# A 4-layer decoder step on one core: the residual given turned and loaded in eight pieces, and GLA's sample states as moving operand

## The chip, the cores and the metric

The kernel runs on one core of a Trainium2 chip. Its time is device microseconds (us) of one launch; the median of three runs is given. The engines are TensorE (PE; its weight loads are PEld), VectorE (DVE), ScalarE (ACT), GpSimd (POOL) and SyncE (SP), which issues most of the DMAs.

## What is computed

One inference step of a hybrid decoder for a prompt of 1024 tokens and a sample group of 8 sequences with 8 new tokens each, 1088 tokens in all, of width 1024. Layer 0 runs HGRN2 and latent attention beside each other, layer 1 gated linear attention (GLA); an MLP follows each. Everything is float32. The two places that the change touches are the input of the first projection and the GLA scan:

```python
hp = rmsnorm(xp, norm_mix[layer]); hs = rmsnorm(xs, norm_mix[layer])
hq, hf, hi, hg, cq, ckv, kr = _split(h @ w_in, EVEN_SPLIT)        # layer 0

def step(S, inp):                                                 # GLA, layer 1
    qb, kb, vb, gb = inp
    b = jnp.cumsum(gb, axis=2)
    o_inter = jnp.einsum('bhtk,bhkv->bhtv', qb * jnp.exp(b), S)
    ...
    o = o_inter + jnp.einsum('bhts,bhsv->bhtv', scores, vb)
    S_new = jnp.exp(b_last)[..., None] * S + jnp.einsum('bhsk,bhsv->bhkv', k_dec, vb)
```

For the sample group `S` comes in as `state_gla`: for each of 8 sequences and 4 heads a state of 128 keys by 256 values, met by the 8 queries of that sequence.

## The kernel before

The program is a row of stages, each with its own buffers and semaphores and a barrier of all engines at its end: load, even (the first projection), latent, attention, mix (HGRN2 and the sample attention), output projection, MLP, odd (the second projection), gla, output projection, MLP, store. Within a stage each engine has its own list of instructions, written out by hand, and waits on semaphores.

**The residual** lives on chip as `K.xT`, turned: 128 partitions by 8 pieces k by 1088 tokens. `load_stage` fetches the tokens row by row in nine tiles, on SP and ScalarE in turn, turns each in eight 128x128 pieces on TensorE, and ScalarE and VectorE copy them out. At the start of the even stage SP stores `K.xT` to DRAM as `K.x_save`, because the stage reuses its room for the latents; the output projection fetches it back.

**The first projection** multiplies in three parts: weights and x are split into a rounded high part and a low rest. ScalarE makes `x_hi` piece by piece (`high(act, k)`), VectorE `x_lo`. The first weight tile is in `K.first`, fetched during the load stage by `load_following`; the second, `raw[1]` (even_raw in the trace), is issued by SP as the first thing of the even stage. ScalarE splits it between `high` of k = 2 and k = 3. `first_two_groups` runs the first two groups of 128 outputs side by side, the second three pieces behind the first, and puts the sums of squares for the norm (`norm.pe`) in between. They need all seven additions on VectorE (`own.add`).

**GLA** runs four heads. In pass p (0 to 4) TensorE does the eight levels of head p, one a slot, each eight products of 128x128 (`level`, bank HB), and in the same slots the outputs of head p - 1: the values in slots 0 to 3, the sample values in slot 4, keys and state updates of the samples in slot 5, values turned and means in slot 6. In pass 4 there are no levels, and the sample values stand in slot 0. Small results share a ring of five PSUM banks, in the order of `banks_in_order`. The sample values of a head are, for each half of the 256 values, one product for the new tokens and eight with the states:

```python
for bi in range(NB):
    t = slice(bi * TS, (bi + 1) * TS)
    end = pe.matmul(out[:, t], s0[:, h % 2, bi, of], q_dec[:, SEQ + bi * TS:SEQ + (bi + 1) * TS],
                    start=False, stop=(bi == NB - 1))
```

Here the state is the stationary operand, 128x128, and 8 queries are the moving columns.

Of the kernel before, what the change touches and what calls it, by code (L numbers as in the profile page):

```python
# [20 lines left out]
ACT = mybir.ActivationFunctionType  # L21
# [3 lines left out]
P = 128  # L25
D = 1024
KD = D // P
# [105 lines left out]
def load_stage(nc, K, following):  # L133


    TILES = 9

    def rows(tile):
        return P if tile < 8 else NS

    with Stage(nc, "load") as s:
        xin = s.sb("xin", [P, TILES, D])
        tp = [s.ps(f"tp{i}", [P, 4, P]) for i in range(4)]
        const_in, ident_in, xin_in = s.sem("const_in"), s.sem("ident_in"), [s.sem(f"xin_in{i}") for i in range(TILES)]
        turned, following_in = s.sem("turned"), s.sem("following_in")
        copied_lo, copied_hi = s.sem("copied_lo"), s.sem("copied_hi")
        block = s.block()
        xp, xs = K.x_prompt, K.x_sample

        def fetch(eng, tile):  # L150
            src = xp[tile * P:(tile + 1) * P, :] if tile < 8 else xs
            eng.dma_start(xin[0:rows(tile), tile, :], src).then_inc(xin_in[tile], 16)

        @block.sync
        def _(sp):
            fetch(sp, 0)
            for tile in range(2, TILES, 2):
                fetch(sp, tile)
            load_following(sp, K, following, following_in)
            sp.wait_ge(following_in, 16)  # L160

        @block.gpsimd
        def _(pool):
            pool.memset(K.ones[:], 1.0)
            pool.memset(K.eps[:], EPS)
            with nc.allow_non_contiguous_dma(reason="a column of each norm weight, once"):
                for n, w in enumerate([K.norm_mix[0], K.norm_mlp[0], K.norm_mix[1], K.norm_mlp[1]]):
                    pool.dma_start(K.norms[:, n, :], w.rearrange("(k p) -> p k", p=P)).then_inc(const_in, 16)
            pool.wait_ge(const_in, 4 * 16)

        @block.tensor
        def _(pe):
            pe.wait_ge(ident_in, 16)
            for tile in range(TILES):
                n, i = rows(tile), tile % 2
                pe.wait_ge(xin_in[tile], 16)
                for half in range(2):
                    if tile >= 2:
                        pe.wait_ge(copied_lo if half == 0 else copied_hi, tile - 1)
                    for k in range(4):  # L180
                        c = (4 * half + k) * P
                        last = pe.transpose(tp[2 * i + half][:, k, 0:n], xin[0:n, tile, c:c + P], K.ident[0:n, 0:n])
                    last.then_inc(turned, 1)
            pe.wait_ge(copied_hi, 8)
            keep_running(pe, K, tp[3][:, 0, :], 4)

        def copy_out(eng, copy, half, copied):
            for tile in range(TILES):
                n = rows(tile)
                eng.wait_ge(turned, 2 * tile + half + 1)  # L190
                copy(K.xT[:, 4 * half:4 * half + 4, tile * P:tile * P + n], tp[2 * (tile % 2) + half][:, :, 0:n]
                     ).then_inc(copied, 1)

        @block.scalar
        def _(act):
            act.dma_start(K.ident[:], K.c_ident).then_inc(ident_in, 16)
            for tile in range(1, TILES, 2):
                fetch(act, tile)
            copy_out(act, lambda o, x: act.activation(o, x, ACT.Copy), 0, copied_lo)
# [4014 lines left out]
```

## Time and profile before

| | |
|---|---|
| median of three runs | 3082.57 us (3078.41 to 3083.43) |
| profiled execution | 3076.06 us, span 3074.3 us |
| mean TensorE clock | 0.989 of full speed |
| TensorE busy | 2978.1 us, 97% of the span |
| VectorE, ScalarE, GpSimd busy | 53%, 41%, 53% |
| moved by DMA | 451.91 MB, mean 147 GB/s |
| load stage | up to about 22 us |
| GLA stage | about 2076 to 2245 us |

The profile is of one execution. Times in it are from the start of the span; the time of the execution is the span and 1.8 us around it. A float32 matmul shows as two passes of TensorE, so counts of matmuls in the trace are twice those in the order of instructions, except for the turns against the identity. A clock of 1.00 is 2.4 GHz and 0.50 is 1.2 GHz.

### The profile page before, as it was taken

Reading aid. Unit: us, or ns where it says so; the run is one execution under the profiler, and the core shown is the slowest. Engines: PE = TensorE matmul, PEld = TensorE weight load, DVE = VectorE, ACT = ScalarE, POOL = GpSimd, SP = SyncE. Lnnn points to the kernel's source line nnn. Section 1 sums busy time; section 2 is a strip of 40 time slices with the busy share of each in tenths; the row PEclk is TensorE's granted clock in tenths of the full one; section 3 lists DMA queues with packets and bytes.
Section 4 is the critical chain, followed back from the end, with each engine's and each line's share of the span. In section 5 each row is a group of like instructions: output and inputs, shape, how many; then the busy total and the mean of one; then the engine's idle time right before and its main releaser. Section 6 shows DMA issues by size and latency. Waiting matters only on the chain. (4 is left out here: it accounts for less than half of the span.)

```text
span 3074.3 us, 55978 instructions
## 1 busy us (share of the span) xinstructions
PE 2978.1 (97%) x22805; PEld 2769.3 (90%) x22805; DVE 1631.1 (53%) x2254; ACT 1263.9 (41%) x2187; POOL 1639.1 (53%) x1375
## 2 busy tenths in 40 slices
PE   8999999999999999998999999999999999989998
PEld 7999667777777999998999989998899999989998
DVE  4122465566554374547666626734445644576665
ACT  4111435656654344344444452312444334344443
POOL 1122103455441167878999715731111687789995
PEclk9999999999999999999999999999999999999999
DMA  6222204667663134446344134657541444454442
GB/s 225 56 81 75 65 28 161 213 231 243 220 251 108 49 112 153 143 133 218 136 152 146 43 127 149 227 205 281 200 123 45 142 145 133 152 200 141 144 144 80
DMA packets 298127, 451.91 MB, mean 147 GB/s; under 512 B 18545, under 2 KB 195633, under 8 KB 297617
## 3 DMA queue, kind: packets, MB, share of 16 engines
q1 hardware_dynamic: 277152, 357.54, 34.6%
q0 software_dynamic: 20000, 88.64, 8.3%
q8 instruction: 182, 2.98, 0.4%
q10 hardware_dynamic: 720, 2.16, 0.2%
q14 instruction: 73, 0.59, 0.1%
HBM read 318.47 MB, written 129.81 MB: 146 GB/s over the span
## 5 line engine op out<-in xcount | busy, mean ns | idle before, releaser
L112 PE MATMUL mlp_X<-mlp_f_hi,mlp_w_hi 128*128 128x272 f32 x1968 | 568.7, 289 | 15.8 <-DVE xT L965 14.0
L113 PE MATMUL mlp_X<-mlp_f_lo,mlp_w_hi 128*128 128x272 f32 x1968 | 568.9, 289 | 0.0
L114 PE MATMUL mlp_X<-mlp_f_hi,mlp_w_lo 128*128 128x272 f32 x1968 | 568.1, 289 | 0.0
L809 POOL TENSOR_TENSOR mlp_w_lo<-mlp_raw,mlp_w_hi 128x256 fp32r<-128x256 f32 (+1 forms) x348 | 344.2, 996 | 162.2 <-ACT mlp_w_hi L693 120.8
L112 PEld LDWEIGHTS mlp_X<-mlp_f_hi,mlp_w_hi 128*128 128x128 f32 x1968 | 371.6, 189 | 18.4 <-DVE xT L965 16.3
L113 PEld LDWEIGHTS mlp_X<-mlp_f_lo,mlp_w_hi 128*128 128x128 f32 x1968 | 372.0, 189 | 0.0
L114 PEld LDWEIGHTS mlp_X<-mlp_f_hi,mlp_w_lo 128*128 128x128 f32 x1968 | 371.7, 189 | 0.0
L809 POOL TENSOR_TENSOR mlp_w_lo<-mlp_sums,mlp_w_hi 128x256 fp32r<-128x256 f32 (+1 forms) x276 | 299.7, 1086 | 14.5 <-ACT mlp_w_hi L693 11.1
L112 PE MATMUL mlp_Z<-mlp_f_hi,mlp_w_hi 128*128 128x272 f32 x976 | 281.3, 288 | 3.8 <-ACT mlp_ev L732 2.2
L113 PE MATMUL mlp_Z<-mlp_f_lo,mlp_w_hi 128*128 128x272 f32 x976 | 281.5, 288 | 0.0
L114 PE MATMUL mlp_Z<-mlp_f_hi,mlp_w_lo 128*128 128x272 f32 x976 | 281.0, 288 | 0.0
L965 DVE TENSOR_TENSOR xT<-xT,mlp_X 128x544 f32<-128x544 f32 x256 | 184.1, 719 | 141.6 <-PE mlp_X L114 140.2
L693 ACT ACTIVATE mlp_w_hi<-mlp_raw 128x256 fp32r<-128x256 f32 (+1 forms) x340 | 158.7, 469 | 207.9 <-PE mlp_X L114 125.0
L693 ACT ACTIVATE mlp_w_hi<-mlp_sums 128x256 fp32r<-128x256 f32 (+1 forms) x276 | 130.4, 480 | 228.9 <-POOL mlp_sums L809 128.5
L112 PEld LDWEIGHTS mlp_Z<-mlp_f_hi,mlp_w_hi 128*128 128x128 f32 x976 | 183.5, 188 | 5.0 <-ACT mlp_ev L732 2.6
L112 PE MATMUL odd_bank<-odd_x_hi,odd_w_hi 128*128 128x352 f32 (+1 forms) x552 | 181.5, 329 | 5.4 <-POOL odd_w_lo L3025 5.4
L113 PEld LDWEIGHTS mlp_Z<-mlp_f_lo,mlp_w_hi 128*128 128x128 f32 x976 | 183.8, 188 | 0.0
L114 PEld LDWEIGHTS mlp_Z<-mlp_f_hi,mlp_w_lo 128*128 128x128 f32 x976 | 183.6, 188 | 0.0
L114 PE MATMUL odd_bank<-odd_x_hi,odd_w_lo 128*128 128x352 f32 (+1 forms) x552 | 180.8, 327 | 0.0
L113 PE MATMUL odd_bank<-odd_x_lo,odd_w_hi 128*128 128x352 f32 (+1 forms) x552 | 180.6, 327 | 0.0
L112 PE MATMUL even_bank<-even_x_hi,even_w_hi 128*128 128x352 f32 (+1 forms) x504 | 166.3, 330 | 0.4 <-DVE even_w_lo L1312 0.4
L114 PE MATMUL even_bank<-even_x_hi,even_w_lo 128*128 128x352 f32 (+1 forms) x504 | 165.0, 327 | 0.0
(577 smaller groups left out, 7598.2 us busy)
## 6 DMA issues: line engine op xcount, KB each, us to landing
hidden<-mlp_ev SPq DMA_DIRECT2D x224, 272.0 KB, 2.2
mlp_f_lo_plain<-hidden SPq DMA_DIRECT2D x112, 544.0 KB, 5.5
mlp_raw<-in_w_down SPq DMA_DIRECT2D x64, 512.0 KB, 3.5
mlp_raw<-in_w_up SPq DMA_DIRECT2D x48, 512.0 KB, 5.6
projections<-odd_zout SPq DMA_DIRECT2D x24, 544.0 KB, 4.2
forms<-gla_f SPq DMA_DIRECT2D x20, 544.0 KB, 2.7
residual<-xT SPq DMA_DIRECT2D x2, 4352.0 KB, 15.1
projections<-even_zout SPq DMA_DIRECT2D x16, 544.0 KB, 3.2
```

What stands on the lines that cost most here:

```text
L112: pe.matmul(out, w_hi, x_hi, start=first, stop=False, skip_group_check=onto)
L113: pe.matmul(out, w_hi, x_lo, start=False, stop=False, skip_group_check=onto)
L114: return pe.matmul(out, w_lo, x_hi, start=False, stop=last, skip_group_check=onto)
L693: act.activation(slot(i)[0], src, ACT.Copy).then_inc(whi_done, 1)
L809: pool.tensor_tensor(to, x, y, op).then_inc(done_by, 1)
L965: dve.tensor_tensor(dst, dst, read_x(bank), ALU.add).then_inc(added, 1)
```

## The change

1. `kernel()` gives two more inputs: `x_turned`, the tokens laid out as `K.xT` is, and `c_norms`, the norm weights as columns. The load stage no longer turns anything. SP and ScalarE issue the eight pieces of 544 KB straight into `K.xT`, each with a semaphore of its own (`K.x_in[k]`) that the even stage takes over and waits for before `high(act, k)`. The first weights are issued first on SP and waited for in the even stage.
2. `K.x_save` is not written for the first layer; the output projection fetches from `x_turned` instead.
3. In GLA the operands of the sample states change places. `sample_queries` takes 32 columns of queries as stationary operand (8 of the sequence, 24 that follow and are not used) and the state's 256 values as moving ones. Four sequences go into the four quarters of a bank's partitions, eight matmuls in all. ScalarE copies the bank to `o_turned`, and `sample_values` turns and adds it with four matmuls against rows of the identity.

```diff
 def load_stage(nc, K, following):
     with Stage(nc, "load") as s:
...
+        const_in, filled = s.sem("const_in"), s.sem("filled")
+        K.first_in, K.x_in = s.carried("first_in"), [s.carried(f"x_in{k}") for k in range(KD)]
         block = s.block()
+        def fetch(eng, k):
+            eng.dma_start(K.xT[:, k, :], K.x_turned[:, k, :]).then_inc(K.x_in[k], 16)
 
         @block.sync
         def _(sp):
-            fetch(sp, 0)
-            for tile in range(2, TILES, 2):
-                fetch(sp, tile)
-            load_following(sp, K, following, following_in)
-            sp.wait_ge(following_in, 16)
+            load_following(sp, K, following, K.first_in)
+            for k in range(1, KD, 2):
+                fetch(sp, k)
+
+        @block.scalar
+        def _(act):
+            act.dma_start(K.norms[:], K.c_norms).then_inc(const_in, 16)
+            fetch(act, 0)
+            act.dma_start(K.ident[:], K.c_ident).then_inc(const_in, 16)
+            for k in range(2, KD, 2):
+                fetch(act, k)
+            act.wait_ge(const_in, 32)
...
-        @block.tensor
-        def _(pe):
-            pe.wait_ge(ident_in, 16)
-            for tile in range(TILES):
-                n, i = rows(tile), tile % 2
-                pe.wait_ge(xin_in[tile], 16)
...
@@ even_stage
             load(1)
-            sp.dma_start(K.x_save, K.xT[:]).then_inc(saved, 16)
...
+            act.wait_ge(K.first_in, 16)
             first.high(act, 0)
             for k in range(KD):
                 if k == 2:
                     first.high(act, 1)
                 if k == 3:
                     act.wait_ge(raw_in[1], 16)
                     split(1)
+                act.wait_ge(K.x_in[k], 16)
                 high(act, k, xhi_done)
...
@@ gla_stage
+                if p and i == sample_slot(p):
+                    uses.append((("oq", p - 1, 0), "A"))
                 if p and 0 <= i - value_slot(p, 0) < 4:
                     uses.append((("o", p - 1, i - value_slot(p, 0)), "A"))
...
+            def sample_queries(h):
+
+                b = bank(("oq", h, 0))
+                pe.wait_ge(cleared, 3)
+                pe.wait_ge(q_in, 16 * h + 16)
+                pe.wait_ge(s0_in, 16 * h + 16)
+                for m in range(2):
+                    for j in range(4):
+                        t0 = SEQ + (4 * m + j) * TS
+                        end = pe.matmul(b[QW * j:QW * (j + 1), m * V:(m + 1) * V], q_dec[:, t0:t0 + QW], s0[:, h % 2, 4 * m + j, :],
+                                        start=True, stop=True)
+                end.then_inc(filled, 1)
+
             def sample_values(h):
                 b = bank(("os", h, 0))
                 pe.wait_ge(a_out, L * h + L)
-                pe.wait_ge(q_in, 16 * h + 16)
-                pe.wait_ge(s0_in, 16 * h + 16)
+                wait_read(pe, ("oq", h, 0))
+                own_rows = K.ident[:].rearrange("p (j n) -> p j n", n=QW)[:, :, 0:TS]
                 for vc in range(VC):
                     out, of = b[:, vc * NS:(vc + 1) * NS], slice(vc * P, (vc + 1) * P)
                     pe.matmul(out, v_tok[0:NS, C, of], a[0:NS, h % 2, C, 0:NS], start=True, stop=False)
-                    for bi in range(NB):
-                        t = slice(bi * TS, (bi + 1) * TS)
-                        end = pe.matmul(out[:, t], s0[:, h % 2, bi, of], q_dec[:, SEQ + bi * TS:SEQ + (bi + 1) * TS],
-                                        start=False, stop=(bi == NB - 1))
+                    for m in range(2):
+                        end = pe.matmul(out[:, m * 4 * TS:(m + 1) * 4 * TS].rearrange("p (j n) -> p j n", n=TS), o_turned[:, m, of],
+                                        own_rows, start=False, stop=(m == 1))
                 end.then_inc(filled, 1)
...
+            def queries_out(h):
+                wait_filled(act, ("oq", h, 0))
+                if h:
+                    wait_filled(act, ("os", h - 1, 0))
+                act.activation(o_turned[:].rearrange("p m v -> p (m v)"), bank_of(("oq", h, 0))[:], ACT.Copy).then_inc(read_act, 1)
...
-                sp.dma_start(K.xT[:, SLOT[k], :], K.x_save[:, SLOT[k], :]).then_inc(x_back, 16)
+                sp.dma_start(K.xT[:, SLOT[k], :], K.x_turned[:, SLOT[k], :]).then_inc(x_back, 16)
```

The order of instructions on SP at the start of the program, before (xin are the token tiles, first the first weight tile):

```order
L152 DMA load_xin<-in_x_prompt 128x1024 x4
L152 DMA load_xin<-in_x_sample 64x1024
L371 DMA first<-in_w_in_even 128x8x128
L74 UNCONDITIONAL_BRANCH [waits load_following_in]
L1206 UNCONDITIONAL_BRANCH [waits barrier_Pool_Activation_PE_DVE_SP_release]
L1214 DMA even_raw<-in_w_in_even 128x8x128
L1224 DMA residual<-xT 128x8704
```

and of the change:

```order
L330 DMA first<-in_w_in_even 128x8x128
L141 DMA xT<-in_x_turned 128x1088 x4
L74 UNCONDITIONAL_BRANCH
L1166 UNCONDITIONAL_BRANCH [waits barrier_Pool_Activation_PE_DVE_SP_release]
L1174 DMA even_raw<-in_w_in_even 128x8x128
L1174 DMA first<-in_w_in_even 128x8x128 [waits even_lo_done]
```

The weights moved ahead of the tokens, even_raw follows four pieces of x in one queue, and the store of the residual is gone. ScalarE in the same place, of the change (w_hi is the high part of a weight tile):

```order
L319 ACTIVATE even_w_hi<-first 128x512 [waits load_first_in]
L297 ACTIVATE even_x_hi<-xT,norms 128x1088 [waits load_x_in0]
L297 ACTIVATE even_x_hi<-xT,norms 128x1088 [waits load_x_in1]
L319 ACTIVATE even_w_hi<-first 128x512
L297 ACTIVATE even_x_hi<-xT,norms 128x1088 [waits load_x_in2]
L1207 ACTIVATE even_w_hi<-even_raw 128x1024 [waits even_raw_in1]
L297 ACTIVATE even_x_hi<-xT,norms 128x1088 [waits load_x_in3]
```

The order is as it was; each piece now has a wait of its own. TensorE in GLA, around the last head's sample values, before (k_tok and v_own make the state updates):

```order
L3357 MATMUL gla_HB<-gla_f 128x128 x8
L3390 MATMUL gla_R<-gla_v_tok,gla_k_tok 128x256 x8
L3414 MATMUL gla_R<-gla_a,gla_v_tok 128x64
L3417 MATMUL gla_R<-gla_q_dec,gla_s 128x8 x8
L3414 MATMUL gla_R<-gla_a,gla_v_tok 128x64
L3417 MATMUL gla_R<-gla_q_dec,gla_s 128x8 x8
L3425 MATMUL gla_R<-gla_v_own,gla_k_tok 128x512 x4
```

and of the change, first around an inner head's, then around the last one's:

```order
L3380 MATMUL gla_R<-gla_s,gla_q_dec 32x256 x8
L3321 MATMUL gla_HB<-gla_f 128x128 x8
L3391 MATMUL gla_R<-gla_a,gla_v_tok 128x64
L3393 MATMUL gla_R<-ident,gla_o_turned 128x32 x2
```

```order
L3354 MATMUL gla_R<-gla_v_tok,gla_k_tok 128x256 x8
L3380 MATMUL gla_R<-gla_s,gla_q_dec 32x256 x8
L3391 MATMUL gla_R<-gla_a,gla_v_tok 128x64
L3393 MATMUL gla_R<-ident,gla_o_turned 128x32 x2
L3391 MATMUL gla_R<-gla_a,gla_v_tok 128x64
L3393 MATMUL gla_R<-ident,gla_o_turned 128x32 x2
L3401 MATMUL gla_R<-gla_v_own,gla_k_tok 128x512 x4
```

A level product (HB) stands between queries and values in the inner heads, and nothing in the last.

## Rows read from the trace of the kernel before

**Rows 1.** The page: span and busy time.

```profile
span 3074.3 us, 55978 instructions
PE 2978.1 (97%) x22805; PEld 2769.3 (90%) x22805; DVE 1631.1 (53%) x2254; ACT 1263.9 (41%) x2187; POOL 1639.1 (53%) x1375
```

**Rows 2.** Stretches: length, busy by engine PE to POOL, clock, DMA share, GB/s.

```profile
2.00:20.00 18.00, 10.61 (x65) 9.55 (x66) 4.84 (x7) 5.87 (x9) 3.02 (x4) 1.00 0.94 278
46.43:51.46 5.03, 5.03 (x15) 3.80 (x16) 0.00 (x0) 1.92 (x3) 2.15 (x1) 0.66 0.01 3
```

**Rows 3.** Timeline of SP's queue (start us, us, engine, line): first weights.

```profile
3.52 0.61 SPq L371 DMA_DIRECT2D first<-in_w_in_even  x1
```

**Rows 4.** DMA issues of the first 24 us: KB, us to landing.

```profile
first<-in_w_in_even SPq DMA_DIRECT2D x1, 512.0 KB, 16.8
...
even_raw<-in_w_in_even SPq DMA_DIRECT2D x1, 512.0 KB, 4.3
```

**Rows 5.** Timeline of ScalarE, 22 to 56 us; in brackets idle before.

```profile
22.73 0.63 ACT L360 ACTIVATE even_w_hi<-first 128x512 fp32r<-128x512 f32 x1 [1.93 <-PEq L76]
...
27.08 1.04 ACT L1249 ACTIVATE even_w_hi<-even_raw 128x1024 fp32r<-128x1024 f32 x1
28.02 5.57 ACT L338 ACTIVATE even_x_hi<-xT,norms 128x1088 fp32r<-128x1088 f32 x5
...
51.69 0.31 ACT L309 ACTIVATE even_rstd<-even_sum,eps 128x64 f32<-128x64 f32 x1 [2.13 <-PE even_sum L301]
```

**Rows 6.** Timeline of VectorE, 22 to 56 us.

```profile
30.51 1.22 DVE L1312 TENSOR_TENSOR even_w_lo<-even_raw,even_w_hi 128x1024 fp32r<-128x1024 f32 x1
...
36.70 9.68 DVE L332 TENSOR_TENSOR acc<-acc,even_sq 128x1088 f32<-128x1088 f32 x7
54.47 1.88 DVE L1329 TENSOR_TENSOR even_zout<-even_bank,even_rstd 128x384 f32<-128x384 f32 x4 [8.10 <-ACT even_rstd L312]
```

**Rows 7.** Timeline of TensorE, 42 to 64 us: the first sums.

```profile
46.43 2.41 PE L301 MATMUL even_sum<-acc,ones 128*128 128x512 f32 x4 [2.49 <-DVE acc L332]
```

**Rows 8.** Stretches of GLA from each head's sample values on, columns as before.

```profile
2120.89:2130.38 9.49, 9.49 (x54) 9.28 (x53) 0.70 (x1) 0.45 (x2) 2.44 (x1) 0.64 0.18 59
2163.09:2171.00 7.91, 7.91 (x53) 7.75 (x53) 0.70 (x1) 0.45 (x2) 2.48 (x1) 0.78 0.50 198
2203.72:2212.72 9.00, 9.00 (x63) 8.64 (x62) 1.41 (x2) 0.89 (x3) 2.48 (x1) 0.81 0.20 64
2226.75:2239.62 12.87, 12.87 (x74) 10.76 (x73) 9.80 (x15) 6.15 (x8) 1.46 (x2) 0.73 0.32 119
```

**Rows 9.** Timeline of TensorE in GLA, head 1's sample values and after.

```profile
2163.09 0.43 PE L3414 MATMUL gla_R<-gla_a,gla_v_tok 64*128 64x64 f32 x2
2163.46 1.95 PE L3417 MATMUL gla_R<-gla_q_dec,gla_s 128*128 128x8 f32 x16
2165.34 0.43 PE L3414 MATMUL gla_R<-gla_a,gla_v_tok 64*128 64x64 f32 x2
...
2167.51 3.66 PE L3357 MATMUL gla_HB<-gla_f 128*128 128x128 f32 x16
2171.00 1.15 PE L3369 MATMUL gla_R<-ident,gla_k_dec 128*128 128x128 f32 x9
```

**Rows 10.** Timeline of TensorE in GLA: another level product.

```profile
2139.05 1.95 PE L3357 MATMUL gla_HB<-gla_f 128*128 128x128 f32 x16
2140.84 1.46 PE L3390 MATMUL gla_R<-gla_v_tok,gla_k_tok 128*128 128x256 f32 x6
```

**Rows 11.** Timeline of TensorE in the first output projection.

```profile
956.63 0.64 PE L3840 MATMUL evenout_A<-mla_acc,evenout_sel 128*32 128x256 f32 x8
957.20 0.64 PE L3842 MATMUL evenout_A<-mla_rows_new,evenout_pnT 64*32 64x256 f32 x8
```

**Rows 12.** Lines L3840 and tile gla_R: ns of one, min/median/max.

```profile
L3840 PEld LDWEIGHTS evenout_A<-mla_acc,evenout_sel x8: 106/108/109, 956.6 to 956.7; 128*32 128x32 f32 x8
L3840 PE MATMUL evenout_A<-mla_acc,evenout_sel x8: 379/391/403, 956.6 to 956.9; 128*32 128x256 f32 x8
...
L3498 ACT ACTIVATE gla_v_tok<-gla_R x16: 591/602/617, 2087.1 to 2218.7; 128x512 f32<-128x512 f32 x16
```

More of the change, by code:

```diff
@@ L133, in load_stage @@
 def load_stage(nc, K, following):
-    TILES = 9
-    def rows(tile):
-        return P if tile < 8 else NS
     with Stage(nc, "load") as s:
[L142 to L146, printed above, removed]
+        const_in, filled = s.sem("const_in"), s.sem("filled")
@@ L162, in _ @@
+        @block.scalar
[6 more added lines that the diff above has]
+            act.wait_ge(const_in, 32)
         @block.gpsimd
         def _(pool):
[L164 to L168, printed above, removed]
@@ L169, in _ @@
-            pool.wait_ge(const_in, 4 * 16)
-        @block.tensor
-        def _(pe):
-            pe.wait_ge(ident_in, 16)
-            for tile in range(TILES):
-                n, i = rows(tile), tile % 2
-                pe.wait_ge(xin_in[tile], 16)
[L177 to L199, printed above, removed]
@@ L201, in _ @@
-        @block.vector
-        def _(dve):
-            copy_out(dve, lambda o, x: dve.tensor_copy(o, x), 1, copied_hi)
+            pool.memset(K.ones[:], 1.0).then_inc(filled, 1)
+            pool.memset(K.eps[:], EPS).then_inc(filled, 1)
+            pool.wait_ge(filled, 2)
 def store_stage(nc, K):
@@ L1194, in even_stage @@
         M.z_stored = [16 * len(STORED[i::2]) for i in range(2)]
-        saved, following_in, const_in, weight_in = (s.sem(n) for n in ("saved", "following_in", "const_in", "weight_in"))
+        following_in, const_in, weight_in = (s.sem(n) for n in ("following_in", "const_in", "weight_in"))
         lat_squared, lat_added, lat_mean, lat_logged, lat_rstd, lat_normed = (s.sem(n) for n in (
@@ L1240, in _ @@
                 store(g - 2)
-            sp.wait_ge(saved, 16)
             sp.wait_ge(const_in, 16 * 8)
@@ L1319, in evacuate @@
                 if g in LATENT:
-                    if c == 0 and g == LATENT[0]:
-                        dve.wait_ge(saved, 16)
                     dst = K.xT[:, g - LATENT[0], t0:t0 + tn]
@@ L3115, in gla_stage @@
     ITEMS, FB, RB = L + 1, G.FB, 5
+    QW = 32
     K_DEC, Q_DEC = len(LEVELS), len(LEVELS) + 1
@@ L3436, in _ @@
                 for i in range(SLOTS):
+                    if p and i == sample_slot(p):
+                        sample_queries(p - 1)
                     if p < HEADS:
@@ L3515, in roots @@
                 act.activation(rstd[:], rstd[:], ACT.Exp, scale=-0.5).then_inc(rstd_out, 1)
+            def queries_out(h):
[3 more added lines that the diff above has]
+                act.activation(o_turned[:].rearrange("p m v -> p (m v)"), bank_of(("oq", h, 0))[:], ACT.Copy).then_inc(read_act, 1)
             for p in range(HEADS + 1):
                 for i in range(SLOTS):
+                    if p and i == sample_slot(p):
+                        queries_out(p - 1)
                     if p and 0 <= i - value_slot(p, 0) < 4:
@@ L4166, in constants, with turned_tokens, norm_columns @@
                 c_unit=(i % 32).astype(f)[:, None])
+def turned_tokens(x_prompt, x_sample):
+    rows = np.concatenate([x_prompt[0], x_sample.reshape(NS, D)])
+    return rows.reshape(T, KD, P).transpose(2, 1, 0)
+def norm_columns(norm_mix, norm_mlp):
+    return np.stack([norm_mix[0], norm_mlp[0], norm_mix[1], norm_mlp[1]]).reshape(4, KD, P).transpose(2, 0, 1)
 OUTPUTS = dict(y_prompt=(1, SEQ, D), y_sample=(NB, TS, D), mla_rows_prompt=(1, 1, SEQ, LAT),
@@ L4206 @@
     nc = bacc.Bacc("TRN2", target_bir_lowering=False, num_devices=1)
-    arrays = {f"in_{n}": np.ascontiguousarray(x) for n, x in {**inputs, **constants()}.items()}
+    arrays = {f"in_{n}": np.ascontiguousarray(x) for n, x in {
+        **inputs, **constants(), "x_turned": turned_tokens(inputs["x_prompt"], inputs["x_sample"]),
+        "c_norms": norm_columns(inputs["norm_mix"], inputs["norm_mlp"])}.items()}
     a = {n[3:]: nc.dram_tensor(n, x.shape, mybir.dt.from_np(x.dtype), kind="ExternalInput").ap()
```

12 lines of the change are left out of this document (6 added, 6 removed).

## The prediction

> **What bounds the kernel now.** I read the page first: TensorE is busy for 2978 of 3074.3 us [rows 1]. So a change counts only where TensorE waits, runs at the lower clock, or has instructions removed. Then I read the timeline and the DMA queues of the first 56 us, and the GLA stage by timeline and by stretches: the two places that the diff touches.
>
> The profiled execution took 3076.06 us, 6.5 us under the median 3082.57 of the runs shown. I sum against it and take the difference off the median. A measurement of this kernel can tell about 0.2%, 6.2 us, from no change.
>
> The start is bound by transfers: from 2 to 20 us the DMA engines are 0.94 busy at 278 GB/s [rows 2], and the first weights, issued last, land at 3.52 + 16.8 = 20.3 us [rows 3, 4]. ScalarE begins the projection at 22.73 us, splits the second weight tile at 27.08 and from 28.02 us makes x_hi for k = 3 and on [rows 5]. From there VectorE has no gap: w_lo to 31.73, x_lo, then seven additions from 36.70 to 46.38 us [rows 6]. TensorE waits 2.49 us for the last of them, until 46.43 us [rows 7]. The five microseconds behind that wait have a mean clock of 0.66: 3.4 us of them at 1.2 instead of 2.4 GHz [rows 2]. The root follows the 64-column sum at their end (Ln at 51.69, VectorE again at 54.47) [rows 5, 6].
>
> In GLA nothing waits at the sample states. But the stretches that hold them, 9.49, 7.91, 9.00 and 12.87 us long and fully busy, have mean clocks of 0.64, 0.78, 0.81 and 0.73 [rows 8]. In head 1 the sample values take 2163.09 to 2167.51 = 4.42 us: twice two passes for the new tokens and 16 passes of 8 moving columns (a matmul in fp32 is two passes in the trace). The level product behind them, 16 passes, takes 3.49 us [rows 9] where it takes 1.79 elsewhere [rows 10]. TensorE is occupied there but streams few columns, and the lower clock follows.
>
> **Start, part by part.** Removed: 72 transposes and 18 copies. They lie under the transfers and are worth nothing in themselves. The 4352 KB store of the residual goes too; nothing on TensorE waited for it: 0.
> Moved: the eight pieces of the residual and the first weights are issued from the first microsecond, and the projection takes each as it lands. Two places of the order matter. On SP the second weight tile (even_raw) is issued behind the first weights and four pieces. On ScalarE the split of that tile stands ahead of x_hi for k = 3. So k = 0, 1 and 2 go early, and everything from k = 3 on waits for even_raw, the last tile of the whole load.
> When does it land? By 20.3 us 64 + 4352 + 512 KB were in. Now 528 KB more stand ahead of its end (the tile itself, and the norms in one piece): 540,672 B / 278 GB/s = 1.9 us, so 22.2 us. GpSimd's gather of the norms leaves the same engines; no row prices it alone, and I allow 0.3 us: 21.9. Bounds: 20.3 if the longer rows move that much faster, and 24.6 if the tile starts only when all else is in and then takes the 4.3 us that it takes now [rows 4].
> The split then starts at 22.0 instead of 27.08 us [rows 5]. The chain behind it, ScalarE's x_hi and VectorE's x_lo and additions, keeps its spacing: **5.1 us** (2.4 to 6.7 by the bounds).
> The new wait leaves TensorE idle from about 15 to 24 us; queued behind it are the rest of both groups and the sums. I expect it back at 1.2 GHz. Between 31.73 and 43.94 us (46.43 - 2.49) it has 12.2 us of work at full clock [rows 6, 7]. If it loses what it loses behind the present wait, half of 3.4 us, the 2.49 us wait for the additions covers that. Most of that wait is then gone, and I take the drop of the clock behind it as gone too: 5.03 x (1 - 0.66) = **1.7 us**. Its other end is 0.
>
> **GLA, part by part.** Out of each head go 32 passes of 8 columns. In come eight matmuls with 32 stationary and 256 moving columns, a copy on ScalarE, and four matmuls of 32 columns against the identity.
> The output projection has the same shape as the eight: 128*32 by 256 over the four quarters of the array's columns, eight passes, start to start 956.63 to 957.20 = 0.57 us [rows 11]. Eight matmuls are 16 passes: 1.14 us. The four narrow ones are eight passes with a full stationary tile; nearest are the 8-column ones, 16 in 1.88 us, 0.117 each: 0.94. The new tokens' stay at 4.42 - 2 x 1.88 = 0.66 [rows 9]. Sum 2.74 against 4.42: 1.7 us a head, **6.7 us**.
> The copy of 512 columns takes 0.60 us [rows 12]. For heads 0 to 2 a level product of 1.79 us stands between queries and values and hides it. The last head has none, as the order rows show: there the copy costs its 0.60 and two handovers, which I estimate at 0.2 each: **-1.0 us** (0.6 to 1.4). Behind the waiting TensorE stand the state updates and the last values; VectorE and ScalarE wait for those. The ring of five banks gets one more user a head; the banks behind it keep their predecessors: 0. The fill of 24 columns on GpSimd at the stage's start lies under the first loads: 0.
> Clock: lost time is length x (1 - clock): 3.4 + 1.7 + 1.7 + 3.5 = 10.3 us [rows 8]. The run of few columns shrinks from 4.42 to 1.60 us (0.94 + 0.66) with a level product on either side, so I take the losses of heads 0 to 2 as gone (6.8). In the last head a wait of 1.0 us, narrow matmuls and updates of 32 rows follow one another; there I take half, 1.7. Together **8.5 us**, bounds 0 and 10.3.
>
> One rule speaks against the eight matmuls. The Trainium skill (TensorE: Matmul & The Clock Gate, "The mechanism") says that a weight load overlaps matmuls in flight only where its row group differs, and these share one. The trace disagrees for this shape: eight passes with their loads took 0.57 us, and eight loads of 108 ns in a row would be 0.86 [rows 11, 12]. By the row the four heads save 6.7 us, by the rule nothing.
>
> **Sum.** 5.1 + 1.7 + 6.7 - 1.0 + 8.5 = 21.0 us. 3076.1 - 21.0 = 3055.1 for a profiled execution; 3082.6 - 21.0 = 3061.6, say **3062 us**, for the median.
>
> **Rivals.**
> 1. *The clock still falls behind the sample values.* For it: eight narrow passes remain, and in head 0 the clock was down for most of its 9.49 us [rows 8]. Against: the run is 2.8 times shorter. Gain 21.0 - 8.5 = 12.5: 3070 us. Chance 0.15.
> 2. *The start gives little.* The tile lands at 24.6 us and the cold restart outlasts its cover: 2.4 us and no clock back. Gain 2.4 + 14.2 = 16.6: 3066 us. For it: the tile is last in the longer of two queues. Chance 0.15.
> 3. *Loads not hidden in the narrow tiles*: 16 x 0.108 = 1.7 us a head [rows 12], which eats what is saved. Gain 21.0 - 6.9 = 14.1: 3068.5 us. Chance 0.04. This is the mechanism of the skill's rule named above.
> 4. *Slower.* The array empties between the column quarters, so each of the 16 passes costs its full 0.39 us [rows 12]: 6.3 instead of 1.14 us a head, -20.5 in all, and sparse streaming keeps the lower clock, -8.5. That gives -8.0: 3090.6 us. It decides from a pass of 0.26 us on, where 12.5 us are spent. The 0.57 us for eight stands against it. Chance 0.02.
> 5. *More*: the last head keeps 2.4 GHz too, and the tile lands at 20.3: 21.0 + 1.8 + 1.6 = 24.4: 3058 us. Chance 0.12.
> The forecast itself has 0.52.
>
> **How the numbers follow.** The time is the forecast's, 3062; its own range, with the spread of the runs (3078.4 to 3083.4), is 3058 to 3066. Eight in ten takes in rivals 2, 3 and 5 and about half of 1: 3055 to 3070. All cases but rival 4 gain over 6.2 us: faster 0.94 with something unseen allowed for, 0.04 within, 0.02 slower.
>
> **What would show it.** Right: the split of even_raw at about 22 us with a DMA as its releaser; TensorE's wait ahead of the first sum under 1.5 us and the clock at 1.00 behind it; 16 passes of 32 by 256 in about 1.1 us; a wait of about 1 us for the copy in the last head alone; the level product behind the sample values 1.8 us long in heads 0 to 2. Wrong: even_raw after 24 us; clocks under 0.9 behind the sample values; TensorE waiting elsewhere in GLA, since each head now needs its items, gate and queries some 3 us sooner.

## The result and the profile after

| | before | after |
|---|---|---|
| median of 5 runs | 3082.48 us (3078.41 to 3083.43) | 3065.70 us (3063.49 to 3069.54) |
| ratio, 95% interval | | 0.9946 (0.9934 to 0.9958) |
| profiled execution | 3076.06 us | 3069.54 us |

The change made the kernel 16.8 us faster; 21 were forecast. The profiled execution of after is the slowest of its five runs, so the two profiles lie only 6.5 us apart. The page of after:

```profile
span 3067.8 us, 55744 instructions
...
PE 2965.6 (97%) x22693; PEld 2749.4 (90%) x22693; DVE 1624.0 (53%) x2245; ACT 1264.4 (41%) x2182; POOL 1635.5 (53%) x1372
```

TensorE's busy time fell by 12.5 us [rows 1], its passes from 22,805 to 22,693: four heads lose 32 narrow ones and gain 16 and 8, 32 fewer in all, and most of the rest are the load's 72 turns.

The start, after. SP's queue:

```profile
0.75 0.44 SPq L330 DMA_DIRECT2D first<-in_w_in_even  x1
...
9.09 0.38 SPq L1174 DMA_DIRECT2D even_raw<-in_w_in_even  x1
```

Stretches, as in [rows 2]:

```profile
4.00:14.00 10.00, 4.71 (x20) 4.74 (x21) 2.54 (x3) 4.89 (x6) 2.42 (x3) 1.00 1.04 407
22.00:24.00 2.00, 2.00 (x8) 1.81 (x7) 2.00 (x3) 2.00 (x3) 0.00 (x0) 0.50 0.00 0
24.00:26.00 2.00, 2.00 (x12) 2.00 (x11) 2.00 (x3) 2.00 (x3) 0.00 (x0) 0.84 0.00 0
38.00:40.00 2.00, 2.00 (x3) 0.94 (x4) 0.00 (x0) 0.70 (x2) 2.00 (x1) 0.57 0.00 0
40.00:42.00 2.00, 2.00 (x5) 1.04 (x4) 0.00 (x0) 0.98 (x2) 0.12 (x1) 0.58 0.00 0
```

ScalarE, VectorE (additions, then the copying out of the even stage) and TensorE (the sums), in this order:

```profile
18.62 1.06 ACT L1207 ACTIVATE even_w_hi<-even_raw 128x1024 fp32r<-128x1024 f32 x1 [3.80 <-DMA even_raw<-in_w_in_even]
19.58 5.56 ACT L297 ACTIVATE even_x_hi<-xT,norms 128x1088 fp32r<-128x1088 f32 x5
```

```profile
28.25 9.67 DVE L291 TENSOR_TENSOR acc<-acc,even_sq 128x1088 f32<-128x1088 f32 x7
46.12 2.75 DVE L1287 TENSOR_TENSOR even_zout<-even_bank,even_rstd 128x384 f32<-128x384 f32 x6 [8.20 <-ACT even_rstd L271]
```

```profile
37.98 3.52 PE L260 MATMUL even_sum<-acc,ones 128*128 128x512 f32 x4 [1.92 <-DVE acc L291]
```

The same ten microseconds of the kernel before:

```profile
4.00:14.00 10.00, 6.11 (x29) 5.69 (x30) 1.81 (x3) 2.77 (x4) 1.02 (x2) 1.00 1.00 306
```

The transfers run at 407 GB/s where they ran at 306; from 2 to 20 us it is 339 against the 278 of [rows 2]. ScalarE takes even_raw at 18.62 us, a DMA its releaser; before it was 27.08 [rows 5]. The additions come 8.45 us earlier (28.25 for 36.70) and the copying out 8.35 us, 46.12 for 54.47 [rows 6]. TensorE still waits 1.92 us ahead of the sums, for 2.49 [rows 7]. It also comes back from its wait for the tile at the lower clock (0.50 from 22 to 24 us) and runs at it again from 38 to 42.

GLA, after: TensorE around the sample states of an inner head.

```profile
2123.02 1.07 PE L3380 MATMUL gla_R<-gla_s,gla_q_dec 128*32 128x256 f32 x16
2124.02 2.05 PE L3321 MATMUL gla_HB<-gla_f 128*128 128x128 f32 x16
2126.00 0.43 PE L3391 MATMUL gla_R<-gla_a,gla_v_tok 64*128 64x64 f32 x2
2126.36 0.63 PE L3393 MATMUL gla_R<-ident,gla_o_turned 128*128 128x32 f32 x4
...
2127.76 2.03 PE L3321 MATMUL gla_HB<-gla_f 128*128 128x128 f32 x16
2129.62 0.27 PE L3333 MATMUL gla_R<-ident,gla_k_dec 128*128 128x128 f32 x1
```

The 16 passes of queries take 2123.02 to 2124.02 = 1.00 us, own tokens and narrow passes 2126.00 to 2127.76 = 1.76. The level product behind them takes 1.86 us where it took 3.49 [rows 9]. The stretches of the inner heads from each one's queries on, and two of the last head's end:

```profile
2123.00:2133.00 10.00, 10.00 (x81) 7.82 (x81) 2.36 (x5) 3.34 (x8) 2.49 (x1) 1.00 0.49 163
2160.00:2170.00 10.00, 10.00 (x83) 7.87 (x81) 1.96 (x4) 3.16 (x7) 2.50 (x1) 1.00 0.81 296
2198.00:2208.00 10.00, 10.00 (x81) 7.76 (x80) 2.30 (x4) 3.28 (x8) 2.50 (x1) 1.00 0.19 57
2230.00:2235.00 5.00, 3.79 (x34) 3.60 (x33) 2.27 (x4) 2.40 (x5) 0.00 (x0) 1.00 0.61 210
2235.00:2240.00 5.00, 3.78 (x18) 3.81 (x19) 3.48 (x4) 3.80 (x5) 0.00 (x0) 0.66 0.38 110
```

The clock is whole in the heads where it fell to 0.64, 0.78 and 0.81 [rows 8], and falls once at the very end. The last head's copy, with ScalarE's row between TensorE's:

```profile
2219.79 1.07 PE L3380 MATMUL gla_R<-gla_s,gla_q_dec 128*32 128x256 f32 x16
...
2221.03 0.58 ACT L3499 ACTIVATE gla_o_turned<-gla_R 128x512 f32<-128x512 f32 x1
...
2221.75 0.40 PE L3391 MATMUL gla_R<-gla_a,gla_v_tok 64*128 64x64 f32 x2 [0.89 <-ACT gla_o_turned L3499]
```

TensorE waits 0.89 us for it.

To see where the rest went, I read the same anchors in every trace: the starts of the first and last matmul on a stage's tile. Lengths in us. "before" and "changed" are means of three profiles each, "later split" of three kernels with that edit (experiment 4):

| stretch | before | changed | later split |
|---|---|---|---|
| start to the query latents | 301.3 | 293.1 | 289.3 |
| to the first keys of the mix | 195.6 | 196.7 | 196.6 |
| mix | 440.6 (439.0 to 442.3) | 446.9 (445.7 to 448.1) | 441.9 (440.6 to 443.7) |
| to the even output | 7.4 | 7.1 | 7.1 |
| to the odd projection | 821.1 | 823.6 | 822.6 |
| to GLA | 310.3 | 310.7 | 310.1 |
| GLA, to the output's first matmul | 172.2 | 159.1 | 159.1 |
| to the last store's turns | 819.1 | 819.2 | 818.4 |

Two places gain, 8.2 and 13.1 us. The attention mix, whose code is the same, gives 6.3 us back, and the stretch to the odd projection 2.5. The mean spans of the profiled executions, 3076.2 and 3065.8 us, lie 10.4 us apart; the medians show 15 to 17.

### The profile page after: what moved, and what is told of

Its sections match the earlier page's. It is cut to its first block and busy times, and to the rows that moved or that the text cites. A ratio compares the mean times of both kernels' runs of the same rounds, so it can differ in the third digit from the quotient of the medians.

```text
span 3067.8 us, 55744 instructions
## 1 busy us (share of the span) xinstructions
PE 2965.6 (97%) x22693; PEld 2749.4 (90%) x22693; DVE 1624.0 (53%) x2245; ACT 1264.4 (41%) x2182; POOL 1635.5 (53%) x1372
## 5 line engine op out<-in xcount | busy, mean ns | idle before, releaser
L112 PE MATMUL mlp_X<-mlp_f_hi,mlp_w_hi 128*128 128x272 f32 x1968 | 569.1, 289 | 13.5 <-DVE xT L924 11.6
L112 PEld LDWEIGHTS mlp_X<-mlp_f_hi,mlp_w_hi 128*128 128x128 f32 x1968 | 371.8, 189 | 16.0 <-DVE xT L924 13.9
```

The lines of the kernel that those rows point to most:

```text
L112: pe.matmul(out, w_hi, x_hi, start=first, stop=False, skip_group_check=onto)
```

## The experiments

All times are medians. Each group was run on one chip beside the kernel before.

**1. The two halves of the change, each alone, and sample states split in two.** The kernel before took 3078.59 us here.

gla_only is the kernel before with the change's parts in `gla_stage` alone:

```diff
+    o_turned = s.sb("o_turned", [P, 2, V])
...
+                        sample_queries(p - 1)
...
+                        queries_out(p - 1)
```

> Only the GLA part of the change; load and projection as before. In the changed kernel's profile the GLA stage (first level product to the last) is 12 us shorter, 6 of it instructions and 6 to 8 clock. Theory A (the parts add up, and what is missing from the whole is a number of drops of the clock elsewhere that differs by execution, 1.7 us each): 12 us under before, 3070.5, with 0.00 to 3 drops in the mix stage. Theory B (the shift of the start causes the drops of the clock in mix): 12 us as well, but with mix at a clock of 1.00 as in the profile of before, since nothing ahead of GLA moved.

Measured: 3068.80 us, ratio 0.9969 (0.9957 to 0.9981), so -9.8 us (-13.2 to -5.8). GLA is 159.6 us long, 0.6 more than with the whole change. The mix is 442.2 us long and has two drops of the clock, at 589 and 811 us, although nothing ahead of GLA moved. That speaks against Theory B.

start_only is the rest: turned residual, pieces and waits, with GLA as before:

```diff
+            load_following(sp, K, following, K.first_in)
+            for k in range(1, KD, 2):
+                fetch(sp, k)
```

> Only the start of the change (turned residual in pieces, norms as columns); GLA as before. VectorE's first evacuation was at 46.12 us instead of 54.47 in the changed kernel, 8.4 us sooner. Theory A: 8.4 us under before on the median, 3074, with the drops of the clock in mix in some executions only. Theory B: the profile again has the three drops of the clock in mix about 115 us apart and the time is only 1 to 4 us under before, 3078 to 3081.

Measured: 3073.89 us, ratio 0.9983 (0.9973 to 0.9992), so -4.7 us (-8.3 to -2.5), between the two theories. Its even stage copies out at 44.50 us, 10 us earlier than in the first profile of before, which has the drop of the clock behind the sums, and 8 us earlier than in the two without it (experiment 3). The mix is 443.5 us long, with one drop, at 910 us. GLA keeps its 171.1 us and shows how the old form loses the clock. Head 1's two groups of 16 passes of 8 columns in its trace:

```profile
2157.70 1.95 PE L3375 MATMUL gla_R<-gla_q_dec,gla_s 128*128 128x8 f32 x16
...
2160.17 3.58 PE L3375 MATMUL gla_R<-gla_q_dec,gla_s 128*128 128x8 f32 x16
```

The first group takes 1.95 us, the second 3.58: the clock has halved in it. The two halves add to -14.5 us and the whole change gave -15.0 to -16.8: within these intervals they add up.

halves is the kernel before, with the old narrow passes, but the groups of the two value halves on either side of a level product in heads 0 to 2. It changes no instruction, only their order:

```diff
-            def sample_values(h):
+            def sample_values(h, halves=(0, 1)):
...
-                for vc in range(VC):
+                for vc in halves:
...
+                    if 0 < p < HEADS and i == sample_slot(p):
+                        sample_values(p - 1, (0,))
                     if p < HEADS:
                         level(p, i)
...
-                        sample_values(p - 1)
+                        sample_values(p - 1, (1,) if p < HEADS else (0, 1))
```

> Before, with the 8-column matmuls of the sample states kept, but one half of the values put ahead of the level product of slot 4 and the other behind it, in heads 0 to 2; the last head as before. No instruction fewer. If the drop of the clock behind the sample values comes of the length of the run with few columns (2.2 us now instead of 4.4), the drops of heads 0 to 2 go and the kernel is 5 to 7 us faster. If the number of such matmuls in the stage decides, nothing changes: 0 to 1 us.

Measured: 3078.29 us, ratio 0.9994 (0.9985 to 1.0003): no difference that the time can show. But GLA is 166.6 us long, 4.5 less than before. Head 1 in its trace:

```profile
2165.88 1.95 PE L3417 MATMUL gla_R<-gla_q_dec,gla_s 128*128 128x8 f32 x16
2167.69 2.03 PE L3357 MATMUL gla_HB<-gla_f 128*128 128x128 f32 x16
...
2170.01 1.95 PE L3417 MATMUL gla_R<-gla_q_dec,gla_s 128*128 128x8 f32 x16
2171.82 2.71 PE L3357 MATMUL gla_HB<-gla_f 128*128 128x128 f32 x16
```

```profile
2160.00:2168.00 8.00, 8.00 (x69) 7.62 (x68) 1.96 (x4) 2.17 (x4) 0.00 (x0) 1.00 0.94 326
2168.00:2178.00 10.00, 10.00 (x67) 8.49 (x65) 1.81 (x3) 1.64 (x4) 2.48 (x1) 0.83 0.57 205
```

The drops of heads 0 and 2 are gone with nothing but the order changed, and head 1's stays: the mean clock is 0.83 over the ten microseconds that hold the second group. All four profiles of the old order (three of before, and start_only) have a drop in each inner head. So the order alone moves the drops, as the forecast's argument needs, but this rests on one profile, and it did not work in every head. The time answers the other way: it has neither the 5 to 7 us of the first theory nor the 4.5 us that GLA shows in the profile. The mix was 443.5 us in this profile, with two drops, and 439.0 in the first of before; whether that is the reason, one profile can't tell.

after_again is the changed kernel once more, for a second trace.

> The changed kernel once more, unaltered, for a second profile. Theory A: the drops of the clock in mix (three, about 115 us apart, in the first profile) are fewer or elsewhere, and the span is 1.7 us shorter for each that is gone. Theory B: the same three drops at 580, 692 and 806 us.

Measured: 3067.49 us. GLA is again 159.0 us long. The mix is 448.1 us, with clock drops at 507, 586 and 917 us and one of 6.8 us that ends 4 us into it, where the first profile has them at 581, 694 and 806. So neither the places nor the number are fixed. The even stage copies out at 44.54 us instead of 46.12: the drop behind the sums is absent.

**2. Waiting for the whole load.** turned_whole is the changed kernel whose load stage waits for the first weights and all eight pieces:

```diff
             for k in range(1, KD, 2):
                 fetch(sp, k)
+            sp.wait_ge(K.first_in, 16)
+            for k in range(1, KD, 2):
+                sp.wait_ge(K.x_in[k], 16)
...
+            for k in range(0, KD, 2):
+                act.wait_ge(K.x_in[k], 16)
```

> The changed kernel, but the load stage waits for all eight pieces and the first weights before its barrier. All had landed by 17.4 us in the changed kernel, so the even stage starts at about 18.5 us instead of 9.1, and the split of even_raw comes after three pieces of x_hi, 4.4 us on: 22.9 against 18.6. If waiting for the pieces one by one is worth what that chain says, the evacuation is 4.3 us later than in the changed kernel and the time 4 us longer; if only the laying out counted, the two are equal.

Measured: 3067.07 us, ratio 0.9962 (0.9950 to 0.9974), before at 3078.96 on that chip. ScalarE and the copying out:

```profile
16.88 1.28 ACT L324 ACT_TABLE_LOAD   x1 [16.88 <-PEq L76]
...
22.51 1.05 ACT L1212 ACTIVATE even_w_hi<-even_raw 128x1024 fp32r<-128x1024 f32 x1
```

```profile
49.92 2.74 DVE L1292 TENSOR_TENSOR even_zout<-even_bank,even_rstd 128x384 f32<-128x384 f32 x6 [8.12 <-ACT even_rstd L276]
```

ScalarE starts at 16.88 us, not at 9; even_raw is split at 22.51, 3.9 us later than in the change, and the copying out stands at 49.92, 3.8 us later. So of the 8.35 us that the start gained, the laid out load alone brings 4.5 and the piece-wise waits 3.8; all three profiles compared here have the drop of the clock behind the sums. The time does not show the 3.8 us: 0.9962 (0.9950 to 0.9974) stands against 0.9946 (0.9934 to 0.9958) for the change, and the two intervals overlap.

**3. Second and third profiles of the kernel before.** They are two more executions of the same code, 3078.60 and 3079.21 us.

> The kernel before once more, for a second profile. If the mix stage of 439 us in the first profile of it is its rule, this one has 438 to 440 and the stage is lengthened by the shift of the start. If the number of drops of the clock differs by execution, the stage is 439 plus 1.7 us for each drop that falls in it.

> The kernel before a third time, for one more profile of the mix stage: 438 to 440 us if that length is its rule, else 439 plus 1.7 us for each drop of the clock that falls in it.

Measured: the mix is 442.3 and 440.5 us (439.0 in the first). Neither has a clock drop behind the sums of the start, and the copying out is at 52.42 and 52.88 us, where [rows 6] have 54.47. GLA is 172.7 us in both, with losses in the same four places as [rows 8]. Each has one drop in the mix, at 587 and at 697 us. 439 plus 1.7 us fits the 440.5 of the second and is 1.6 us short of the 442.3, so the drops are not all of the difference.

**4. The split of even_raw behind two more pieces.** late_split is the changed kernel with:

```diff
             for k in range(KD):
...
-                if k == 3:
+                if k == 5:
                     act.wait_ge(raw_in[1], 16)
                     split(1)
...
@@ VectorE, w_lo behind low(k)
-                if k == 3:
+                if k == 4:
```

> The changed kernel with ScalarE's split of even_raw, and VectorE's, behind two more pieces of x. If the tile that lands last holds up all behind it, x_hi for k = 3 and 4 are ready before it lands and the chain of additions ends 2 to 3 us sooner (evacuation at 43 instead of 46.1 us), 2 to 3 us off the time. If TensorE, which then gets its second group later, is the bound, nothing.

Measured: 3059.59 us, ratio 0.9937 (0.9919 to 0.9955). ScalarE and VectorE:

```profile
13.62 3.38 ACT L297 ACTIVATE even_x_hi<-xT,norms 128x1088 fp32r<-128x1088 f32 x3
18.66 1.06 ACT L1207 ACTIVATE even_w_hi<-even_raw 128x1024 fp32r<-128x1024 f32 x1 [1.67 <-DMA even_raw<-in_w_in_even]
```

```profile
25.05 9.68 DVE L291 TENSOR_TENSOR acc<-acc,even_sq 128x1088 f32<-128x1088 f32 x7 [0.28 <-ACT even_sq L285]
41.23 2.74 DVE L1287 TENSOR_TENSOR even_zout<-even_bank,even_rstd 128x384 f32<-128x384 f32 x6 [6.51 <-ACT even_rstd L271]
```

ScalarE now makes three x_hi while the tile is on its way. The tile lands at the same 18.66 us, but the wait for it is 1.67 us, not 3.80. The additions start 3.2 us earlier, the copying out 4.9: the first profile of the change has a drop behind the sums, and no drop falls in the first 350 us of this execution. Against the two profiles of the change without that drop (44.54 and 44.47 us) it is 3.2 to 3.3.

**5. The three side by side.** On one chip, before at 3079.57 us (9 runs), the others with 5 runs each. after_timed is the changed kernel.

> The changed kernel unchanged, as the yardstick of the two kernels beside it on one chip, and a third profile of it. Theory A (what the early start leaves behind in the mix is nothing fixed: it is where the clock's drops happen to fall): the ratio is that already measured, 0.993 to 0.996, the even stage still begins its copying out near 46 us, the sample stage is again 159 us long, and the mix is anywhere from 440 to 448 us. Theory B (the earlier start costs the mix a fixed amount): the mix is again 445 us or more, as in 5 of 5 profiles with the moved start.

Measured: 3064.53 us, ratio 0.9947 (0.9934 to 0.9961). Mix 445.7, GLA 159.2. The 445 us of Theory B hold here, but not "in 5 of 5": the moved start had 443.5 us in start_only and 443.6 in turned_whole and late_split. Stretches and the copying out:

```profile
22.00:24.00 2.00, 2.00 (x8) 2.00 (x7) 2.00 (x3) 2.00 (x2) 0.00 (x0) 0.50 0.00 0
24.00:26.00 2.00, 2.00 (x8) 2.00 (x8) 2.00 (x3) 2.00 (x3) 0.00 (x0) 0.50 0.00 0
38.00:40.00 2.00, 1.98 (x5) 1.02 (x6) 0.00 (x0) 1.97 (x3) 1.70 (x1) 1.00 0.00 0
```

```profile
44.47 2.74 DVE L1287 TENSOR_TENSOR even_zout<-even_bank,even_rstd 128x384 f32<-128x384 f32 x6 [6.50 <-ACT even_rstd L271]
```

The lower clock lasts from 20 to 26 us here, all of it covered, and the clock is whole behind the sums.

late_again is the kernel of experiment 4.

> The kernel with the split of the last tile moved two pieces down, timed beside the changed kernel on one chip. Theory A (the split of the last tile stands ahead of pieces that landed before it, so it holds the even projection up): the copying out of the even stage begins 4 to 5 us earlier than in the changed kernel, near 41.2 us as in its first profile, and the median is 3 to 6 us below the changed kernel's. Theory B (the lower time of its first run was a favourable chip or fewer drops of the clock by chance): the copying out is earlier, but the medians lie within 2 us of each other.

Measured: 3054.55 us (3052.49 to 3057.42), ratio 0.9921 (0.9907 to 0.9935). That is 10.0 us under the changed kernel, more than either theory gave, and all its times lie under the changed kernel's (from 3061.51). The first measurement, against before on another chip, had 0.9937 where the change has 0.9946 and 0.9947: some 3 us. VectorE:

```profile
41.33 2.74 DVE L1287 TENSOR_TENSOR even_zout<-even_bank,even_rstd 128x384 f32<-128x384 f32 x6 [6.54 <-ACT even_rstd L271]
```

The copying out is 3.1 us earlier than in after_timed and 4.8 earlier than in the first profile. Of the 13.3 us between the spans of after_timed (3064.0) and late_again (3050.7), the start has 3.2, the mix 5.1 (440.6 us), and the stretch to the odd projection and the last one 3.1 and 3.4; the others give back 1.5. The lower clock cost 34.0 us in after_timed and 25.9 in late_again, which is 8.1 of the 13.3 us. Why the later split should have fewer drops far behind the start, no run shows; what it does by itself is the 3 us of the start.

best adds to it that the last head's query passes go ahead of its chunk states, and their copy between ScalarE's logarithms and exponential:

```diff
+                if p == HEADS - 1 and i == 7:
+                    uses.append((("oq", p, 0), "A"))
                 uses.extend((("U", p, g), "D") for g in state_groups(p, i))
...
+                    if p == HEADS - 1 and i == 7:
+                        sample_queries(p)
                     if state_groups(p, i):
...
                 wait_read(act, ("m", h, NC - 1))
+                if h == HEADS - 2:
+                    queries_out(HEADS - 1)
```

> The kernel before it with, besides, the last head's 16 sample passes issued ahead of its chunk states, and their copy between ScalarE's logarithms and the exponential behind them, so that TensorE no longer waits for the copy. Theory A (that wait, 0.9 us, is on the path to the odd projection's output): the wait ahead of the last head's sample products is gone, the sample stage is 158 us long and the time 1 us below that of the kernel with the later split, which a time alone can hardly show. Theory B (TensorE waits for ScalarE's logarithms and the passes' banks instead, or the later exponential holds up VectorE's normalisation and with it the last values): the stage stays at 159 us or grows to 160.

Measured: 3057.55 us (3056.42 to 3059.83), ratio 0.9928 (0.9915 to 0.9942). ScalarE's copy, TensorE and the stretch behind:

```profile
2208.84 0.60 ACT L3505 ACTIVATE gla_o_turned<-gla_R 128x512 f32<-128x512 f32 x1
```

```profile
2205.34 1.07 PE L3382 MATMUL gla_R<-gla_s,gla_q_dec 128*32 128x256 f32 x16
...
2207.97 2.86 PE L3356 MATMUL gla_R<-gla_v_tok,gla_k_tok 128*128 128x256 f32 x12 [0.50 <-ACT gla_rstd L3494]
2210.76 0.43 PE L3393 MATMUL gla_R<-gla_a,gla_v_tok 64*128 64x64 f32 x2
```

```profile
2208.00:2222.00 14.00, 14.00 (x84) 11.60 (x85) 11.90 (x20) 10.37 (x15) 1.47 (x2) 0.88 0.40 153
```

The wait for the copy is gone: no idle time ahead of 2210.76. GLA is 158.8 us, and 159.0 to 159.3 in the five other profiles of the change and the later split: at most 0.5 of the 0.9 us arrived, between the two theories. A second clock drop now falls among the last values (0.88 over 14 us). The whole is 3.0 us slower than late_again. Between these two profiles (spans 3058.1 and 3050.7) the time lost to the lower clock, summed as length x (1 - clock) over the span, is 32.9 against 25.9 us. That is 7.0 of the 7.4 us. The kernel of experiment 4, without the moved queries, is the fastest here.

## Why the prediction was right, step by step

**Start, 5.1 us forecast, 8.4 measured.** The mechanism was right: the even stage hangs on even_raw, released by its DMA, and everything behind keeps its spacing (9.63 us from the split to the additions, 9.62 before). The size failed in "When does it land?": the transfer was priced at the 278 GB/s of [rows 2]. The same 18 us ran at 339 after, and the ten from 4 to 14 us at 407, where they had 306. The change removed the norms' gather on GpSimd's queue and made the rows of x longer. Which of the two raised the rate was not tried. The lower bound of 20.3 us was too high as well; the tile was there by 18.62. The 0.3 us allowed for the gather is a guess that no run prices.

**Clock behind the sums, 1.7 us forecast.** The step "Most of that wait is then gone" failed: the wait is 1.92 us in the first profile. It is 1.25 and 1.04 us in the next two, since a slower restart at 20 to 26 us pushes work into it. Nor is the term a fixed price: the drop is there in one profile of three of the changed kernel, and in one of three of the kernel before. Over all 13 profiles it does go with the wait, as the forecast assumed. It follows in five of the seven that wait 1.92 to 2.50 us there (before, after, gla_only, halves and turned_whole; not in before_again and before_again2), and in none of the six that wait 0.04 to 1.60 us. The cold restart was there and covered, as forecast.

**GLA's instructions, 6.7 us forecast, 6.6 measured**: queries 1.00 for 1.14, sample values 1.76 for 1.60, together 2.76 against 4.42, 1.66 a head. Eight matmuls of 32 stationary and 256 moving columns cost what [rows 11] said. Rivals 3 and 4 are wrong. The loads are as long as rival 3 had them, 106 to 110 ns each, but hidden:

```profile
L3380 PEld LDWEIGHTS gla_R<-gla_s,gla_q_dec x64: 106/110/110, 2123.0 to 2220.3; 128*32 128x32 f32 x64
L3380 PE MATMUL gla_R<-gla_s,gla_q_dec x64: 379/379/403, 2123.0 to 2220.5; 128*32 128x256 f32 x64
```

Sixteen such loads in a row would be 1.7 us and sixteen passes 6.1, where all of it took 1.00. In the trace the passes start in fours, one for each column quarter, 7 ns apart and a new four every 0.215 to 0.240 us; the loads of a later four start beside passes in flight. So passes of different quarters, and with them the loads, do overlap. The Trainium skill's rule (TensorE: Matmul & The Clock Gate, "The mechanism"), that a load overlaps matmuls in flight only where its row group differs, does not hold for these. The same section also lets a load go ahead into a background weight buffer; whether these loads do that, no row shows.

**The last head's copy, 1.0 us forecast, 0.89 measured**, and none in the inner heads. The copy takes 0.58 us and the handovers 0.17 and 0.14, for 0.2 each.

**GLA's clock, 8.5 us forecast.** I took S, the start of the state updates in each head, as a mark. From the stage's first level product to head 0's S, then from S to S, and from head 3's S to the output's first matmul, before: 54.99, 40.63, 40.64, 18.51 and 16.36 us; after: 50.31, 37.53, 37.53, 17.81 and 15.84. Heads 0 to 2 gained 4.68, 3.10 and 3.11 us, 10.9 in all; 1.66 x 3 = 5.0 of it is instructions, and 5.9 the clock, for 6.8 forecast. The last head gained 1.2 us for 2.4 forecast, and not because TensorE kept its drop. To the end of its last product (the first turn on HB, at 2243.19 us before and 2232.29 after) that head is 3.95 us shorter: 0.7 of it is instructions, with the wait for the copy taken off, and 3.25 the clock, which stays whole as in rival 5. (Not always: gla_only and turned_whole, with the same GLA code, still have the drop there.) What is lost again lies behind. TensorE's next work, the first turns of the output projection, before and after, and the transfer that counts:

```profile
2245.81 2.02 PE L121 MATMUL oddout_mean<-ident 128*128 128x128 f32 x16 [1.12 <-PEq L76]
2236.22 3.54 PE L121 MATMUL oddout_mean<-ident 128*128 128x128 f32 x16 [2.43 <-PEq L76]
out_gla_state_sample<-gla_s POOLq DMA_DIRECT2D x1, 1024.0 KB, 5.0
```

TensorE waits 2.43 us at the barrier for 1.12, and behind that wait the clock is at the lower level, so that the turns take 3.19 us to the first product for 1.78. Together that is 2.7 of the 3.95 us. The barrier now waits for the store of the last head's sample states: GpSimd issues it at 2229.02 us, it lands at 2234.06, and TensorE goes on 2.16 us later. The distance from that landing is 2.15 to 2.16 us in all six profiles of the change and the later split, and 2.96 to 4.07 in the three of before, where ScalarE's last copies come later than the store. This is read from the traces; no run issues the store earlier. The forecast had looked for waits in GLA and not at who ends the stage. The stage gained 12.1 us, 14.2 forecast. Rival 1 is wrong.

**The sum.** 8.4 + 12.1 = 20.5 us is at hand, near the 21.0 forecast, and that is luck: a start term too small by 3.3 us stood beside two clock terms and a stage's end that gave less. The medians show 16.8 and 15.0; 3065.7 lies at the upper edge of the 3058 to 3066 forecast. The missing 3.7 to 5.5 us are in what the forecast didn't speak of, above all the mix. Of the 31 distances there between the products of successive steps, most agree to 0.1 us in all profiles. The 7th, 15th, 23rd and 31st are either 13.9 or 15.6 us, by whether a drop of the clock falls in them: 0, 1 and 1 of the four are long in the three profiles of before, 3, 2 and 2 in those of the changed kernel, and 2, 1 and 1 with the later split. That is about 1.7 x 1.7 = 2.8 of the 6.3 us. Of the other 3.5, 2.3 lie at the start of the mix (the first step takes 9.4 to 13.9 us, 10.4 to 10.6 before, and in two profiles 1.7 us more pass ahead of it) and 1.1 in the 26th step (12.7 to 13.5 us, 12.1 before). It is not a fixed price of an earlier start: the later split starts earlier still, and its mix is 441.9 us. Whether these places lose the clock more often in the changed kernel at all stays open. The old start in gla_only and halves has two long steps each and 442.2 and 443.5 us; the new one in start_only and turned_whole has one each and 443.5 and 443.6. No run here shifts the mix alone.

The half about the start has the shakier gain, then. start_only was worth 4.7 us of its 8.4, gla_only 9.8 of 12.

## What to carry to other kernels

Where a load is consumed piece by piece, look at which tile the consumer's instruction order puts first against the order of landing: moving one split behind two pieces that landed before it gave 3 us where it acts. The time fell by some 3 us in one measurement and by 10 in the other, most of it drops of the clock elsewhere that the split doesn't explain. A run of matmuls with few moving columns was paid twice here, in itself and in the clock of what followed; swapping the operands so that the wide side moves removed both in the inner heads, at the price of a copy that needs other work on TensorE beside it. When TensorE gets through a stage sooner, look at what else the barrier at its end waits for: a store that was covered before took 1.3 us of the gain here, and the clock behind that wait 1.4. When a local gain is well measured and the time shows less, compare the lengths of all stages over several executions before looking for a wait: in one pair of profiles here a 20 us gain showed as 6.5.

## What was not expected of the hardware

- The lower clock comes in portions that cost about 1.7 us each (2 us stretches at 0.50 to 0.66; steps of 13.9 or 15.6 us), and one execution has them where another of the same code has not: behind the sums of the start in one of three, in the mix in 0 to 3 of four places. As length x (1 - clock) over the span they cost 33.5, 36.7 and 40.0 us in three profiles of before. The changed kernel lost 36.8, 40.2 and 34.0, although GLA's part went from 10.2 to 11.9 us to 1.7. So about as much clock was lost elsewhere as GLA won, and why stays open.
- The same 16 passes of 8 columns took 1.95 and 3.58 us in two groups with one pair of passes between them.
- The first transfers reached 407 GB/s over 10 us, 1.3 times what the old load had in the same ten. The old load reached 410 as well, but only in single stretches of 2 us.
- Eight matmuls of 32 stationary columns, spread over the four column quarters, took 1.00 us with their 16 loads of 106 to 110 ns.
